# Attention stages: a pair's turned probabilities leave PSUM in one copy, and a head pair's four value blocks in one

## The reference, cut to what matters

```python
# first layer: 8 heads share one latent of 128 channels as key and as value (dsa)
logits = einsum('bthc,btkc->bthk', qa, kv_sel) + bias         # -inf outside the selection
p = softmax(logits);  o = einsum('bthk,btkc->bthc', p, kv_sel)
# second block, layer 0: 8 heads of 64 with a forget-gate decay (fox)
logits = q k^T + (F[t] - F[s]);  p = softmax(logits);  out = p v
# second block, layer 1: 16 heads, 96 wide for query and key, 64 for value (mla)
logits = q k^T;  p = softmax(logits);  out = p v
```

## Time and profile before

| | us |
|---|---|
| median of 3 runs | 2717.99 (2716.43 to 2718.21) |
| span of the profiled execution | 2715.4 |
| PE busy in it | 2643.5 |
| DVE busy | 1880.0 |
| ACT busy | 1201.3 |

### The profile page before, as it was taken

The page is one execution under the profiler, slowest core; times in us unless marked ns, Lnnn a source line. Parts: engine busy times, 40 slices in busy tenths (PEclk is TensorE's granted clock), DMA queues, the critical chain, the costliest instruction groups (busy, mean ns, idle before and its releaser), DMA issues. The chain is left out here.

```text
span 2715.4 us, 48462 instructions
## 1 busy us (share of the span) xinstructions
PE 2643.5 (97%) x18904; PEld 2251.7 (83%) x18904; DVE 1880.0 (69%) x3435; ACT 1201.3 (44%) x2277; POOL 267.2 (10%) x203
## 2 busy tenths in 40 slices
PE   7999999999999899999999999999999999999998
PEld 4878847788888799998868999989999856899997
DVE  4466767533333788886368888888888767788885
ACT  3243146321212544444265444454444448554444
POOL 1001013420313100003101000010000100100000
PEclk9999989999999999999999999999999999999999
DMA  8142211123222333334212333333332340333331
GB/s 286 58 144 69 93 38 36 62 94 107 94 89 66 93 91 96 96 98 126 78 32 78 107 96 97 99 101 102 94 116 87 78 113 2 94 100 95 97 106 55
DMA packets 363395, 248.87 MB, mean 92 GB/s; under 512 B 28692, under 2 KB 356184, under 8 KB 363168
## 3 DMA queue, kind: packets, MB, share of 16 engines
q1 hardware_dynamic: 362674, 245.18, 30.5%
q10 hardware_dynamic: 494, 0.59, 0.1%
HBM read 241.52 MB, written 2.12 MB: 90 GB/s over the span
## 5 line engine op out<-in xcount | busy, mean ns | idle before, releaser
L3189 ACT CAST dense_wt_hi<-ring 128x512 fp32r<-128x512 f32 x719 | 444.3, 621 | 462.4 <-PE bank L3239 220.5
L3194 DVE TENSOR_TENSOR dense_wt_lo<-ring,dense_wt_hi 128x512 fp32r<-128x512 f32 x719 | 493.9, 689 | 107.7 <-ACT dense_wt_hi L3189 106.3
L3226 PE MATMUL bank<-dense_operand_hi,dense_wt_hi 128*128 128x256 f32 x1248 | 353.7, 283 | 3.9 <-DVE h L3843 3.9
L3228 PE MATMUL bank<-dense_operand_hi,dense_wt_lo 128*128 128x256 f32 x1248 | 353.1, 283 | 0.0
L3227 PE MATMUL bank<-dense_operand_lo,dense_wt_hi 128*128 128x256 f32 x1248 | 353.1, 283 | 0.0
L3239 PE MATMUL bank<-dense_act_hi,dense_wt_hi 128*128 128x512 f32 x832 | 258.4, 392 | 0.8 <-DVE dense_act_lo L3507 0.8
L3239 PE MATMUL bank<-dense_act_lo,dense_wt_hi 128*128 128x512 f32 x832 | 257.2, 390 | 0.0
L3239 PE MATMUL bank<-dense_act_hi,dense_wt_lo 128*128 128x512 f32 x832 | 256.6, 390 | 0.0
L3226 PE MATMUL bank<-feat_hi,dense_wt_hi 128*128 128x256 f32 (+1 forms) x820 | 246.9, 301 | 7.6 <-DVE h L3878 4.1
L3226 PEld LDWEIGHTS bank<-dense_operand_hi,dense_wt_hi 128*128 128x128 f32 x1248 | 238.8, 191 | 11.8 <-issue 4.6
L3228 PE MATMUL bank<-feat_hi,dense_wt_lo 128*128 128x256 f32 (+1 forms) x820 | 246.0, 300 | 0.0
(11 more groups left out here) (739 smaller groups left out, 5345.5 us busy)
## 6 DMA issues: line engine op xcount, KB each, us to landing
ring<-in_ffn_w_up SPq DMA_DIRECT2D x88, 512.0 KB, 3.9
ring<-in_ffn_w_gate SPq DMA_DIRECT2D x88, 512.0 KB, 5.2
ring<-in_ffn_w_down SPq DMA_DIRECT2D x60, 512.0 KB, 4.7
ring<-in_ada_w SPq DMA_DIRECT2D x24, 1024.0 KB, 5.8
ring<-in_ffn_w_down SPq DMA_DIRECT2D x52, 256.0 KB, 3.7
ring<-in_w_ffn_gate SPq DMA_DIRECT2D x11, 1024.0 KB, 5.3
ring<-in_w_ffn_up SPq DMA_DIRECT2D x11, 1024.0 KB, 5.3
ring<-in_w_in SPq DMA_DIRECT2D x8, 1024.0 KB, 5.4
```

The source lines that it names most:

```text
L3189: self.nc.scalar.copy(self.hi(i), src).then_inc(self.s_high, 1)
L3194: self.nc.vector.tensor_tensor(self.lo(i), self.items[i][1], self.hi(i).bitcast(F32), ALU.subtract).then_inc(self.s_low, 1)
L3226: pe.matmul(out, h[:, w], xh, start=start and k == 0, stop=False, skip_group_check=shared)
L3228: last = pe.matmul(out, l[:, w], xh, start=False, stop=stop and k == 3, skip_group_check=shared)
```

## The change

The eight PSUM banks, which were eight tensors, become one tensor of 8 x 512, so that one instruction can name two neighbouring banks. `probs_out` then makes one copy of both items of a pair (banks 4 and 5 into two neighbouring rows of `pt`), after the transposes of both. In fox and mla the value products of the four query blocks of a head pair go side by side into the columns of one bank, and `values_out` copies this bank once per head pair, after the fourth. In dsa `values_out` makes one copy of the two heads' banks per pair. The counts on the semaphores follow: the transposes of an even item wait until the whole previous pair has been copied, those of an odd item wait for no copy of their own.

```diff
         def probs_out(e, copy, j):
-            for m in (2 * j - 4, 2 * j - 3):
-                w = width(m)
-                e.wait_ge(s_turned, m + 1)
-                if m >= 4:
-                    e.wait_ge(s_pv, m // 2 - 1 if shared else 2 * (m // 2) - 2)
-                copy(pt[:, m % 4, 0:w], K.bank[4 + m % 2][:, 0:w]).then_inc(s_pt, 1)
+            g = j - 2
+            m, w = 2 * g, width(2 * g)
+            e.wait_ge(s_turned, m + 2)
+            if g >= 2:
+                e.wait_ge(s_pv, g - 1)
+            copy(pt[:, m % 4:m % 4 + 2, 0:w], K.banks[:, 4:6, 0:w]).then_inc(s_pt, 1)
 
         def values_out(e, copy, g):
-            if shared:
-                h, i = items[2 * g]
+            h, i = items[2 * g]
+            if shared and g % TB == TB - 1:
                 e.wait_ge(s_pv, g + 1)
-                copy(dest(h, i), K.bank[6 + g % 2][:, 0:P]).then_inc(s_out, 1)
-            else:
-                for m in (2 * g, 2 * g + 1):
-                    h, i = items[m]
-                    e.wait_ge(s_pv, m + 1)
-                    copy(dest(h, i), K.bank[6 + m % 2][:, 0:P]).then_inc(s_out, 1)
+                copy(dest(h, slice(0, T)), K.bank[6 + g // TB % 2][:, :]).then_inc(s_out, 1)
+            elif not shared:
+                e.wait_ge(s_pv, g + 1)
+                copy(dest(h, slice(i * P, (i + 1) * P)), K.banks[:, 6:8, 0:P]).then_inc(s_out, 1)
...
                         for m in (2 * j - 4, 2 * j - 3):
                             pe.wait_ge(s_norm, m + 1)
-                            if m >= 2:
-                                pe.wait_ge(s_pt, m - 1)
+                            if m >= 2 and m % 2 == 0:
+                                pe.wait_ge(s_pt, m // 2)
...
                     if j >= 3:
                         g = j - 3
-                        pe.wait_ge(s_pt, 2 * g + 2)
-                        if g >= 2 if shared else g >= 1:
-                            pe.wait_ge(s_out, g - 1 if shared else 2 * g)
+                        pe.wait_ge(s_pt, g + 1)
+                        if not shared and g >= 1:
+                            pe.wait_ge(s_out, g)
+                        elif shared and g >= 2 * TB and g % TB == 0:
+                            pe.wait_ge(s_out, g // TB - 1)
...
-                                    last = pe.matmul(K.bank[6 + g % 2][lo(h):lo(h) + vw, 0:P], v(h, s), pt[:, m % 4, s * P:(s + 1) * P],
-                                                     start=s == 0, stop=s == blocks - 1)
-                            last.then_inc(s_pv, 1)
+                                    last = pe.matmul(K.bank[6 + g // TB % 2][lo(h):lo(h) + vw, i * P:(i + 1) * P], v(h, s),
+                                                     pt[:, m % 4, s * P:(s + 1) * P], start=s == 0, stop=s == blocks - 1)
```

More of the change, by code:

```diff
@@ L158, in __init__ @@
         self.rs = sb("rs", [P, T])
-        self.bank = [ctx.enter_context(nc.psum_tensor(f"bank{i}", [P, 512], F32)) for i in range(8)]
+        self.banks = ctx.enter_context(nc.psum_tensor("bank", [P, 8, 512], F32))
+        self.bank = [self.banks[:, i, :] for i in range(8)]
         self.loaded = [sem(f"chunk_loaded{i}") for i in range(2 * RING)]
@@ L2298, in _ @@
                         g = j - 3
-                        pe.wait_ge(s_pt, 2 * g + 2)
-                        if g >= 2 if shared else g >= 1:
-                            pe.wait_ge(s_out, g - 1 if shared else 2 * g)
+                        pe.wait_ge(s_pt, g + 1)
[3 more added lines that the diff above has]
+                            pe.wait_ge(s_out, g // TB - 1)
                         pair = (2 * g, 2 * g + 1)
-                        blocks = items[2 * g][1] + 1
+                        i = items[2 * g][1]
+                        blocks = i + 1
                         if shared:
@@ L2307, in _ @@
                                     h = items[m][0]
-                                    last = pe.matmul(K.bank[6 + g % 2][lo(h):lo(h) + vw, 0:P], v(h, s), pt[:, m % 4, s * P:(s + 1) * P],
-                                                     start=s == 0, stop=s == blocks - 1)
-                            last.then_inc(s_pv, 1)
+                                    last = pe.matmul(K.bank[6 + g // TB % 2][lo(h):lo(h) + vw, i * P:(i + 1) * P], v(h, s),
+                                                     pt[:, m % 4, s * P:(s + 1) * P], start=s == 0, stop=s == blocks - 1)
                         else:
                             for m in pair:
-                                product(pe, K.bank[6 + m % 2][:, 0:P], [(v(items[m][0], s), pt[:, m % 4, s * P:(s + 1) * P])
-                                                                        for s in range(blocks)]).then_inc(s_pv, 1)
+                                last = product(pe, K.bank[6 + m % 2][:, 0:P], [(v(items[m][0], s), pt[:, m % 4, s * P:(s + 1) * P])
+                                                                               for s in range(blocks)])
+                        last.then_inc(s_pv, 1)
             @block.gpsimd
@@ L2417, in mixer1 @@
             A.rb, A.bucket = ab("rb", [32, 8]), ab("bucket", [32, 640])
-            A.out = [y[:, n, :] for n in range(4)] + [M.cq[:, n, :] for n in range(2)] + [A.wuq[:, n, :] for n in range(2)]
+            A.pairs = [y[:, 0:2, :], y[:, 2:4, :], M.cq[:, :, :], A.wuq[:, :, :]]
+            A.out = [pair[:, n, :] for pair in A.pairs for n in range(2)]
             A.wuv = M.ik[:, :].rearrange("p (h d) -> p h d", h=8)
@@ L2429, in mixer1 @@
             attention_stage(K, "dsa", 8, P, lambda h, i: A.qa[:, h, i * P:(i + 1) * P], lambda h, w: M.ckv[:, 0:w],
-                            lambda h, s: A.ckvt[:, s, :], P, lambda h, i: A.out[h][:, i * P:(i + 1) * P], prep=prep, loads=lambda sp: dsa_value_loads(K, A, sp))
+                            lambda h, s: A.ckvt[:, s, :], P, lambda h, c: A.pairs[h // 2][:, :, c], prep=prep, loads=lambda sp: dsa_value_loads(K, A, sp))
         out1_stage(K, A, y, coef, [M.rkv[:, n, :] for n in range(9)])
@@ L3021, in mixer2 @@
         attention_stage(K, "fox", 8, HD, lambda h, i: B.q[r(h), h // 2, i * P:(i + 1) * P], lambda h, w: B.k[r(h), h // 2, 0:w],
-                        lambda h, s: B.v[:, s, h * 64:(h + 1) * 64], 64, lambda h, i: y[:, 4 + h // 2, i * P:(i + 1) * P],
+                        lambda h, s: B.v[:, s, h * 64:(h + 1) * 64], 64, lambda h, c: y[:, 4 + h // 2, c],
                         bias=lambda h, i: B.mask[:, 384 - i * P:384 - i * P + (i + 1) * P],
@@ L4179, in mla_body @@
     attention_stage(K, "mla", MH, QK, lambda h, i: B.Q[:, h, i * P:(i + 1) * P], lambda h, w: B.K[:, h, 0:w],
-                        lambda h, s: B.V[:, s, h * 64:(h + 1) * 64], 64, lambda h, i: y[:, h // 2, i * P:(i + 1) * P],
+                        lambda h, s: B.V[:, s, h * 64:(h + 1) * 64], 64, lambda h, c: y[:, h // 2, c],
                         bias=lambda h, i: B.mask[:, 384 - i * P:384 - i * P + (i + 1) * P],
```

## The result

The changed kernel takes 2723.3 us (median of 20 runs) against 2718.24 of the kernel before beside it: ratio 1.0018, 95% interval 1.0012 to 1.0024, so 5.1 us slower. The forecast was +4.2 us, 2722.2.

The account below looks back on a forecast made before the run. The prediction took PE to bound the kernel (busy 2643.5 of 2715.4 us). Losses of 2.4 in mla, 1.05 in fox and 0.7 in dsa gave +4.2 us, from 2717.99 to 2722.2, range 2719.3 to 2724.6.

Parts of the forecast that it names:

- What bounds: Whole kernel: PE, busy 2643.5 of 2715.4 us, so only time in which PE stands still counts; ACT has slack.
- What the copies cost: Paired copy of 1024 columns: 1.02 us on ACT, 1.23 on DVE, on the line through the measured shapes.
- rival C: Slower by more than 5.4 us: paired copy at its upper bound, 1.18 us; +6.2, 2724.2 us; chance 0.18.
- B: Only the stage ends cost: paired copy faster, down to 0.86 us, or PE resumes without 0.06; +1.8, 2719.8; chance 0.13.
- Waits removed from PE: Value products on PE: the wait for `s_out` costs nothing while satisfied, so removing it brings 0.
- The stall in mla: 384 wide transposes behind a 512 wide pair, 6 times: PE waits for the late paired copy and loses 0.3 us each.
- Fox: Same place in fox, twice, with the decay product in between: 0.16 us; with the end of 0.9, 1.05 in all.
- dsa: Stall of 0.22 us and 0.6 at the end, less 0.1 for DVE's fewer instructions: 0.7 in all.
- The ends: Stage ends, where no score product covers late copies: 0.9 us in mla, 0.9 in fox, last stall included; dsa 0.6.
- The hidden delays in the middle: ACT's exponentials 0.4 us late, 384 wide copy 0.7 late: costed at nothing, being shorter than the work before their readers.
- rival A: Late copies stall PE in the three attention stages and lengthen their ends: 2720.5 to 2723.4 us, taken as 2722.2; chance 0.66.
- Rival D: Faster: ACT and DVE set the pace, removed instructions count 0.05 and 0.06 us each; -6.1, 2711.9; chance 0.03.

Follow-up runs that it names:

- e9_hybrid2: Against e8: the last two head pairs, not only the last, keep one value copy per block; ratio 0.9997 to the kernel before.
- e7_swap: Against the changed kernel: the two waits ahead of an even item's transposes exchanged, copy's wait first; mla 84.90 us against 85.25.
- e1: Against the changed kernel: one early probability copy per item again, gathered values kept; ratio 1.0006 to the kernel before.
- e3: Against the changed kernel: two copies per pair, both after all its transposes, each freeing its own bank; mla 84.46 us against 85.25.
- e2: Against the changed kernel: paired probability copy kept, one value copy per block (per head in dsa) again; ratio 1.0007 to the kernel before.
- e4: Against the changed kernel: two early probability copies, but the even item's transposes wait for both of the previous pair; mla 83.36 us against 85.25.
- e8: Against the kernel before: mla and fox pair copies narrower than 512 and gather values, both outside the last head pair; ratio 1.0002.

## Why the prediction was right, point by point

*What bounds.* Right. In e9_hybrid2 fewer instructions on ACT leave the stages as they were; what moves a stage in mla and fox is when PE can go on.

*What the copies cost.* Right to 10 ns, so rival C (1.18 us) fell with its premise, and so did B.

*Waits removed from PE.* Right at 0: in mla and fox, between a stage's start and its end, the intervals between transposes outside the stalls are those of before within 0.03 us.

*The stall in mla.* The mechanism and its six places are right; the size was forecast as 0.3 and is 0.37 in the middle. The term that was too small is the 0.05 us from the end of a copy to PE's load. I took it from the last value product, but the transposes have two waits, and with the copy's wait written second it is 0.12. e7_swap shows 0.05 with the waits exchanged; that takes the stall to 0.31. The other term of the forecast, 0.06 for six transposes from a standstill, was too large: they take 0.85 us against 0.82.

*Fox.* Its middle loses 0.22 at p = 8 (5.79 to 6.01 us from 512 to 256 wide) where 0.16 was forecast; the 0.07 from copy to load is missing here too. The second place is at its end, where the 384 wide transposes come later by the same 0.25 us (2.04 to 2.29) as at p = 8.

*dsa.* Here a step failed. The forecast had a short interval only behind p = 8 and 12, and DVE's shorter work giving back 0.1. DVE is indeed earlier, but its copy starts only after a reciprocal, so p = 3, the first 512 wide pair, is copied late as well, and p = 4 waits:

```profile
421.72 1.22 DVE L2254 COPY dsa_pt<-bank 128x1024 f32<-128x1024 f32 x1
...
423.09 1.06 PE L2294 MATMUL bank<-const,dsa_S 128*128 128x128 f32 x8
```

The copy ends at 422.94, and PE's weight load follows at 423.06. The interval from the transposes of p = 3 to these is 3.26 us, against 3.18 before, 3.17 and 3.15 with release per item (e1, e3), and 3.27 with joint release (e2, e4). Up to p = 8 the stage loses 0.15 instead of gaining 0.1. The stall behind p = 8 costs 0.15 (7.19 to 7.34 us to the 256 wide pair), not 0.22: the 384 wide transposes come 0.53 later, but the odd item no longer waits for a copy of its own behind them. The end, from p = 12 on, loses 0.70 where 0.6 was forecast, and there the forecast rounded its sum down: its own terms, 457.53 + 3 x 0.13 + 0.22 + 0.68 + 0.41 - 458.55, give 0.68.

*The ends.* The number is right, the path is not, and part of it is luck. With its last stall mla's end loses 0.9 us, as forecast. The timeline, against the earlier trace rows:

```profile
2306.52 0.81 ACT L2254 COPY mla_pt<-bank 128x768 f32<-128x768 f32 x1
...
2307.22 0.41 ACT L2376 ACTIVATE mla_S<-mla_S,mla_stat 128x128 f32<-128x128 f32 x1
...
2307.48 0.63 PE L2294 MATMUL bank<-const,mla_S 128*128 128x128 f32 x4 [0.30 <-ACT mla_pt L2254]
...
2308.14 0.59 ACT L2254 COPY mla_pt<-bank 128x512 f32<-128x512 f32 x1
...
2308.87 0.41 PE L2294 MATMUL bank<-const,mla_S 128*128 128x128 f32 x2
```

Counted from the transposes of p = 28 (2296.82 before, 2303.08 now), the last exponentials come 0.66 late, as forecast (0.67). The forecast let this reach the last transposes through the reciprocal and the scaling. But PE is late before that: the transposes of p = 30 stand 0.30 us for the joint copy of p = 29, which starts at 2306.52 behind the gathered copy. This is the 0.7 us delay that the forecast took as covered; at the end no scores cover it. The last transposes then wait for the joint copy of p = 30: the scaling of their first item is over at 2308.69, this copy at 2308.73, and the weight load follows at 2308.84. They come 0.74 late, 0.65 was forecast. Behind them 0.17 is lost where 0.24 was forecast, since the two transposes take 0.41 us and not 0.49. The two differences cancel. Fox's end loses in the same place (1.83 to 2.16 us from the 384 wide to the 256 wide transposes).

e1, e8 and e9 show what the gathered copies do without joint copies at the end. In e1 and e8 the gathered copy of the second last head pair makes the last exponentials late and the last transposes with them, by the path of the forecast; e9 has no such copy, and its ends are 0.2 (fox) and 0.3 us (mla) shorter than e8's.

*The hidden delays in the middle* (exponentials 0.4 late, the 384 wide copy 0.7 late) were costed at nothing, and next to nothing is what they cost in the middle: the transposes of the 256 wide pair, which need both, start 3.62 us after those of the 384 wide pair, against 3.60 before, and the next two intervals are as before.

*The sum.* 2.4 + 1.05 + 0.7 = 4.15 was forecast, 2.77 + 1.15 + 1.00 = 4.92 measured: mla 0.37, fox 0.10 and dsa 0.30 too small. All three errors go the same way, and the time is at the upper edge of what rival A allowed (2723.4).

*Rival D* fell: the 116 instructions removed gave no time back. Of what the Trainium skill says (Perfetto Trace Analysis, Optimizing Scalar/DVE Operations), it is the sentence on an unsaturated engine that causes bubbles on others and may do better with its instructions broken up that fits here: with the probability copies of mla broken up again (e1) the stage is 2.2 us shorter than with the whole change.

## What to carry to other kernels

Before two copies are joined, look for the shortest time between the work that fills a buffer and the next work that wants it back, and compare it with the joint copy from its later start to its end. Here a joined copy on an engine with slack won nothing, and it lost at the one place in a period where the cover is thin, and at the end of a stage, where there is none. If copies are to be joined, join the narrow ones and leave the wide ones and the last rounds alone; here even that brought no time, since the engine that made them had slack.

## What the runs showed of the hardware that was not expected

The order of two waits ahead of one instruction matters when one of them comes late. With the copy's wait written second PE's weight load came 0.12 us after the copy's end (2305.16 to 2305.28), with it written first 0.05 (2293.67 to 2293.72); where the other condition is the late one, exchanging them cost 0.1 (fox, 2.09 to 2.19). In the traces the second wait is a separate instruction of 51 ns ahead of the weight load.

A copy over two PSUM banks costs what its columns cost: 1013 ns for 1024 on ACT and 1221 on DVE, within 7 ns of the line through 128 and 512 columns of one bank.
